# Layer 0's modulation vectors: 48 weight blocks moved from a stage of their own into the two filter stages, with the operands of their matmuls exchanged

## The reference, cut to what matters

```python
def adaln(cvec, w, b):
    m = (jax.nn.silu(cvec) @ w + b)[:, None, :]      # w: 1024 x 6144
    return jnp.split(m, 6, axis=-1)

def hyena_filters(L, lp):                            # L = 256 for the context (C), 512 for the latent (X)
    ...
    h = jnp.sin(freq * (feat @ lp['hy_w1'].astype(f32) + lp['hy_b1'].astype(f32)))
    h = jnp.sin(freq * (h @ lp['hy_w2'].astype(f32) + lp['hy_b2'].astype(f32)))
    h = (h @ lp['hy_w3'].astype(f32) + lp['hy_b3'].astype(f32)).reshape(L, HY_ORDER, 2, HY_WIDTH)
    ...
    taps = taps * lax.rsqrt(jnp.sum(taps * taps, axis=0, keepdims=True) + EPS)
    return jnp.fft.rfft(taps, axis=0)

    for l in range(DEPTH):
        mod = adaln(c, ada_w[l], ada_b[l])
        mod_c = adaln(c_ctx[None, :], ada_w[l], ada_b[l])
        u_c = modulate(rms_norm(ctx, norm1_g[l]), mod_c[0], mod_c[1])
        ...
```

## Time and profile before

| | us |
|---|---|
| median of 3 runs | 5879.87 (5877.63 to 5884.08) |
| the profiled execution | 5873.12 |
| its span, first to last instruction | 5871.3 |
| `stage_ada`, first to last matmul | 19.3 to 117.4 |
| `stage_modulation(0)` | 117.8 to 126.9 |
| filters of C, with the wait for the store | 126.9 to 181.6 |
| filters of X, with the wait for the store | 181.6 to 276.4 |

### The profile page before, as it was taken

One profiled execution on the slowest core, in us unless ns is written; L12 is line 12 of the kernel. 1 busy time (PEld: TensorE's weight loads), 2 busy tenths in 40 slices (PEclk: granted clock), 3 DMA queues, 4 the chain that ended last, 5 costly groups with the idle time before them and its releaser, 6 DMA issues. The chain is left out here.

```text
span 5871.3 us, 69786 instructions
## 1 busy us (share of the span) xinstructions
PE 4953.4 (84%) x23958; PEld 3990.8 (68%) x23958; DVE 4173.0 (71%) x7269; ACT 1841.7 (31%) x3223; POOL 857.5 (15%) x644
## 2 busy tenths in 40 slices
PE   7696737889797869999999778888885679999998
PEld 5385726633575659889888456624764569999997
DVE  1547577768635979999999767667547967676776
ACT  0222312221122753333333211131233733333333
POOL 0000005600000003333333134200000001111110
PEclk9798868999898989999999889989997789999999
DMA  6152317822122669999999467502121367777775
GB/s 225 65 165 75 111 43 274 298 65 65 54 86 90 169 181 386 396 387 400 388 395 391 157 231 269 191 26 82 51 75 52 100 215 272 276 271 277 272 276 189
DMA packets 465588, 1172.70 MB, mean 200 GB/s; under 512 B 225331, under 2 KB 259540, under 8 KB 412438
## 3 DMA queue, kind: packets, MB, share of 16 engines
q1 hardware_dynamic: 373272, 633.88, 32.0%
q0 software_dynamic: 92160, 536.91, 23.9%
HBM read 1106.46 MB, written 64.23 MB: 199 GB/s over the span
## 5 line engine op out<-in xcount | busy, mean ns | idle before, releaser
L2327 POOL DMA_INDIRECT arena<-in_peer_uv,kept x384 | 517.9, 1349 | 3622.1 <-POOLq L2212 1980.2
L232 PE MATMUL psum<-h_hi,u_ring_hi 128*128 128x384 f32 x2048 | 693.6, 339 | 18.4 <-DVE ring_lo L2415 17.9
L232 PE MATMUL psum<-h_hi,ring_lo 128*128 128x384 f32 x2048 | 694.5, 339 | 0.0
L232 PE MATMUL psum<-h_lo,u_ring_hi 128*128 128x384 f32 x2048 | 693.8, 339 | 0.0
L232 PE MATMUL psum<-v_ring_hi,w_hi 128*128 128x512 f32 x1536 | 609.6, 397 | 5.9 <-DVE ring_lo L2420 5.9
L232 PE MATMUL psum<-ring_lo,w_hi 128*128 128x512 f32 x1536 | 603.8, 393 | 0.0
L232 PE MATMUL psum<-v_ring_hi,w_lo 128*128 128x512 f32 x1536 | 600.4, 391 | 0.0
L2420 DVE TENSOR_TENSOR ring_lo<-kept,v_ring_hi 128x1024 fp32r<-128x1024 f32 x256 | 313.8, 1226 | 301.7 <-ACT v_ring_hi L2375 296.5
L2459 DVE SCALAR_TENSOR_TENSOR arena<-arena 128x1024 f32<-128x1024 f32 x384 | 482.1, 1283 | 19.2
L2447 DVE CUSTOM_DVE_ANT_0 arena<-arena 128x1024 f32<-128x1024 f32 x384 | 462.8, 1220 | 29.0 <-DMA arena<-in_peer_uv,kept 28.3
L2387 ACT ACTIVATE w_hi<-arena 128x384 fp32r<-128x384 f32 x256 | 134.7, 526 | 965.3 <-DVE arena L2430 965.3
(11 more groups left out here) (369 smaller groups left out, 10027.7 us busy)
## 6 DMA issues: line engine op xcount, KB each, us to landing
kept<-in_mix SPq DMA_DIRECT2D x312, 512.0 KB, 3.5
kept<-in_peer_u SPq DMA_DIRECT2D x256, 512.0 KB, 5.8
kept<-in_peer_uv SPq DMA_DIRECT2D x256, 512.0 KB, 4.6
kept<-in_ada SPq DMA_DIRECT2D x96, 512.0 KB, 4.4
gate_scratch<-arena SPq DMA_DIRECT2D x12, 4096.0 KB, 20.7
arena<-gate_scratch SPq DMA_DIRECT2D x128, 384.0 KB, 6.0
spec_scratch<-arena SPq DMA_DIRECT2D x4, 2048.0 KB, 8.5
arena<-in_k_dft_x SPq DMA_DIRECT2D x6, 1024.0 KB, 10.2
```

The lines of the kernel that those rows point to most:

```text
L232: done = pe.matmul(out, lhs[x], rhs[y], start=first and j == 0, stop=last and j == 2)
L2327: pool.indirect_dma_start(rows[q % NBUF], None, peer_uv, bass.IndirectOffsetOnAxis(ap=row_id[q % G][:, q // G:q // G + 1], axis=0))\
```

## The change

`stage_ada` is not called any more. For layer 0 its 48 blocks are worked on inside the two filter stages, 24 in each, at named places of TensorE's program (`blocks_beside`): at the beginning 1, behind the first and the second layer 4 each, behind each tile 1, behind the energies of the last tile but one 2, behind spectrum step 2 five, and the rest behind later steps (C: 6 behind step 3; X: one each behind steps 4 to 7). The operands change places: a block's 128 x 128 part is now the stationary operand and `cs` the moving one, with two columns, so each block gives its two columns directly in PSUM bank 7; the copies and the turning matmuls of layer 0 go. The modulation's arithmetic follows the filters and reads PSUM. Its parameters are loaded in the load block, behind the filter weights, and the constants' wait includes them. The wait for C's store goes to DVE's first write of X's spectrum, the wait for X's store into the modulation stage.

```diff
+                load_filter_weights(sp, 0)
+                sp.dma_start(pars, par[0]).then_inc(consts_in.sem, 16)
                 sp.dma_start(fin_g, final_g).then_inc(consts_in.sem, 16)
-                load_filter_weights(sp, 0)
...
-                sp.wait_ge(consts_in.sem, consts_in.at(80))
+                sp.wait_ge(consts_in.sem, consts_in.at(96))
...
             def _(act):
-                act.wait_ge(consts_in.sem, consts_in.at(80))
+                act.wait_ge(consts_in.sem, consts_in.at(96))
...
-        def stage_ada():
+        def pe_ada_column(pe, j):
+
+            k = j % 4
+            pe.wait_ge(loaded[k].sem, loaded[k].at(16 * (j // 4) + 16))
+            for kc in range(KC):
+                last = pe.matmul(ps[:, 7, 2 * j:2 * j + 2], ring[:, k, kc * P:(kc + 1) * P], cs[:, kc, :],
+                                 start=kc == 0, stop=kc == KC - 1)
+            last.then_inc(blocks_done.sem, 1)
...
-            counted_ada()
...
+                if l > 0:
+                    @block.sync
+                    def _(sp):
+                        sp.dma_start(pars, par[l]).then_inc(consts_in.sem, 16)
+                else:
+                    @block.sync
+                    def _(sp):
+                        sp.wait_ge(store_done.sem, store_done.at(0))
...
-                    dve.wait_ge(consts_in.sem, consts_in.at(16))
+                    if l > 0:
+                        dve.wait_ge(consts_in.sem, consts_in.at(16))
...
+                    raw = ada_raw if l > 0 else ps[:, 7, 0:96]
+                    dve.tensor_tensor(mod, raw.rearrange("p (a b) -> p a b", b=2), b, ALU.add)
...
-        def stage_filters(l, s):
+        def stage_filters(l, s, ada_blocks=None):
...
+                    if ada_blocks:
+                        for j in [j for part in ada_blocks.values() for j in part]:
+                            sp.wait_ge(blocks_done.sem, blocks_done.at(j + 1))
+                            sp.dma_start(ring[:, j % 4, :], block_of(order[place[0] + 4 + j])).then_inc(loaded[j % 4].sem, 16)
                     sp.wait_ge(spectrum_made.sem, spectrum_made.at(2 * nt))
...
-                    sp.wait_ge(store_done.sem, store_done.at(32))
+                    if not ada_blocks:
+                        sp.wait_ge(store_done.sem, store_done.at(32))
...
+                    def columns(place):
+
+                        for j in blocks_at(place):
+                            pe_ada_column(pe, j)
+
...
+                    columns("begin")
                     pe.wait_ge(filter_in[0].sem, filter_in[0].at(ready))
                     pe.matmul(ps[0:HID, 4, 0:L], w1[0:EMB, :], feat[0:EMB, :], start=True, stop=True).then_inc(pe_a.sem, 1)
+                    columns("first layer")
                     pe.wait_ge(act_a.sem, act_a.at(1))
                     pe.matmul(ps[0:HID, 5, 0:L], w2[0:HID, :], h1[0:HID, :], start=True, stop=True).then_inc(pe_a.sem, 1)
+                    columns("second layer")
...
+                        columns(("tile", n))
                         if n > 0:
                             energies(n - 1)
+                    columns("last energies")
                     energies(nt - 1)
...
                                 j += 1
+                                columns(("spectrum", j))
...
+                                if j == 0 and ada_blocks:
+                                    dve.wait_ge(store_done.sem, store_done.at(0))
                                 dve.tensor_tensor(stage(o, kt, 0, r), even, odd, ALU.add)
...
-        stage_ada()
+        def blocks_beside(first, tiles, steps):
+            counts = [("begin", 1), ("first layer", 4), ("second layer", 4)]
+            counts += [(("tile", n), 1) for n in range(tiles)] + [("last energies", 2), (("spectrum", 1), 0), (("spectrum", 2), 5)]
+            left = 24 - sum(n for _, n in counts)
+            counts += [(("spectrum", j), left * (j - 2) // (steps - 3) - left * (j - 3) // (steps - 3)) for j in range(3, steps)]
+            counts.append((("spectrum", steps), 0))
+            at = [first + sum(n for _, n in counts[:k]) for k in range(len(counts) + 1)]
+            return {name: range(at[k], at[k + 1]) for k, (name, _) in enumerate(counts)}
         for l in range(DEPTH):
             last = l == DEPTH - 1
-            stage_modulation(l)
             if not last:
-                stage_filters(l, "C")
-            stage_filters(l, "X")
+                stage_filters(l, "C", blocks_beside(0, 2, 4))
+                stage_filters(l, "X", blocks_beside(24, 4, 8))
+                streamed(48, 0)
+                stage_modulation(l)
+            else:
+                stage_modulation(l)
+                stage_filters(l, "X")
             if not last:
                 mixer(l, "C")
                 choose(l, "C")

```

More of the change, by code:

```diff
@@ L402, in _ @@
                 dve.tensor_tensor(cs, cs, cs_sig, ALU.mult)
-        consts_in.add(80)
+        consts_in.add(96)
         act_a.add(1)
@@ L453, in counted_ada @@
             streamed(48, 0)
-        def stage_ada():
[L457 to L474, removed]
-            counted_ada()
+        def pe_ada_column(pe, j):
[5 more added lines that the diff above has]
+            last.then_inc(blocks_done.sem, 1)
         def stage_modulation(l):
             with nc.Block() as block:
-                @block.sync
-                def _(sp):
-                    sp.dma_start(pars, par[l]).then_inc(consts_in.sem, 16)
+                if l > 0:
[6 more added lines that the diff above has]
+                        sp.wait_ge(store_done.sem, store_done.at(0))
                 @block.scalar
@@ L515, in _ @@
                     b = par_of("ada_b").unsqueeze(2).broadcast_to([P, 48, 2])
-                    dve.tensor_tensor(mod, ada_raw.rearrange("p (a b) -> p a b", b=2), b, ALU.add)
+                    raw = ada_raw if l > 0 else ps[:, 7, 0:96]
+                    dve.tensor_tensor(mod, raw.rearrange("p (a b) -> p a b", b=2), b, ALU.add)
                     dve.drain()
@@ L523, in _ @@
                                                      ALU.add, ALU.mult)
-            consts_in.add(16)
+            if l > 0:
+                consts_in.add(16)
             dve_a.add(1)
             act_a.add(1)
-        def stage_filters(l, s):
+        def stage_filters(l, s, ada_blocks=None):
             L = T_OF[s]
@@ L556, in stage_filters, with blocks_at @@
             ready = 80 if l == 0 else 64
+            def blocks_at(place):
+                return ada_blocks[place] if ada_blocks else ()
             MAGIC, TWO_PI = 12582912.0, 2.0 * math.pi
```

## The result

| | median, us | runs | ratio to before, 95% interval |
|---|---|---|---|
| before | 5875.32 (5867.46 to 5895.02) | 8 | |
| after | 5896.21 (5890.82 to 5906.75) | 8 | 1.0036 (1.0024 to 1.0048) |

The change makes the kernel 21 us slower (14 to 28 by the interval), under half a per cent. The forecast was +13 us, 5893, in a range of 5872 to 5908.

The account below looks back on a forecast made before the run. It took TensorE as the engine the filters ahead of layer 0's first norm wait for: 2.0 - 107.6 - 6.5 + 139 - 22.2 + 8 = +12.7 us, so 5880 + 13 = 5893, range 5872 to 5908.

Parts of the forecast that it names:

- Both prices of a block: On TensorE, 16 records of a modulation block take 1.8 us at 2.4 GHz or 3.4 us at 1.2 GHz.
- a busy TensorE was not enough: On TensorE, full moving streams raise the clock; weight loads with two moving columns do not even hold it, despite full busy share.
- The first rival: Clock holds at 2.4 GHz through all 48 blocks, 86 us, and filters' slow parts speed up: -69 us, 5811; chance 6%.
- What went: Ahead of the first norm: 107.6 us before the filters' first matmul and 6.5 us of waiting for C's store go.
- The start: At kernel start, filter weights and parameters landing before the constants are complete add 2.0 us, bounds nothing and 4.
- The number of slow blocks: In both filter stages, about 33 of 48 blocks at 3.4 us and 15 at 1.8 us, together 139 us.
- a sign of being wrong: TensorE waiting for in_ada, the block loads, would prove the forecast wrong; loads were expected to hide, else 4 us once.
- What of it is hidden: Blocks fill TensorE's idle times in the filters of C and X, hiding 22.2 us.
- The neighbours: Filter matmuls beside blocks slow down: C's L579 +2.2, C's last steps +1.6, X's energies +1.1, X's step +3.4; together +8 us.
- the store of X: Ahead of the norm, X's store is still waited for, 11.6 us, with the modulation arithmetic running beside it at no cost.
- "PEclk near 0.5": Sign in the changed profile: granted TensorE clock near 0.5 from about 22 to 55 us, C's beginning, first and second layer.

Follow-up runs that it names:

- the first experiment: The changed kernel with each block's matmuls streaming 128 moving columns, two of cs repeated 64 times, in place of two: 5824.6 us, 0.9917 of before.
- the last experiment: 128 moving columns spread as in the change, plus X's tables behind four block loads, three blocks moved later, half of X's store early: 5806.3 us, 0.9885 of before.
- the third kernel of the table: The changed kernel with the modulation blocks back in their own stage, the rest of the change kept: norm starts at 264.5 us; 5863.6 us, 0.9980 of before.

## Why the prediction was right, point by point

**The number** is in part luck. 5893 was forecast and 5896 measured, but the forecast added 13 us to the 5880 of three runs, and the eight runs of before have 5875; the difference itself was 13 against 21. So the right comparison is that of the sum with the norm's start, 12.7 against 22.0, and it is made here term by term.

**The mechanism** was right. Both prices of a block, read from the turning groups of before, came out: 1.8 and 3.4 us. The argument that a busy TensorE was not enough, from L592's 12.00 us at 0.50, carried over from 65 rows to two columns; the first experiment shows that the width of the stream decides for these blocks. The first rival (6%) was wrong for two columns, and its 69 us are within reach once they are 128: the last experiment has 66 by the norm's start.

**What went** was right within 2 us: the third kernel of the table gives 12 us for what was summed as 13. Of C's store 5.5 us went at the store itself and not 6.5, since TensorE's first block of X starts 1.25 us after the store's issue and not the 0.3 that was estimated for the barrier. But from TensorE's last work in C to the store's issue it was 2.7 us in place of 3.7, so that the whole idle time between C and X went from 10.50 to 3.99, by 6.5 as forecast.

**The start** came 2.1 us later, 2.0 forecast.

**The number of slow blocks** was nearly right: by the starts of the rows the blocks take 142.6 us, 139 forecast. Most of the 3.6 lies in the two groups of five behind step 2, 14.5 us each, in which one or two blocks were fast and not the two or three of the forecast. There was 0.6 us of waiting for a load; such a wait was named as a sign of being wrong, and it showed, but it explains 0.6 us of 22.

**What of it is hidden**, 22.2 us, was right: none of those waits is left, nor one of 0.43 ahead of X's last energies that was not listed. Spreading gave 32.8 in all; the difference is in the main the fast blocks less the slowed neighbours.

**The neighbours** are the term that was too small: 8 forecast. By the starts of the rows C's energies took 12.5 us in place of 8.2 before, X's 20.3 in place of 16.2, C's last two steps 7.3 in place of 5.4 and X's steps 3 and 4, between which no block stands, 2.7 more behind the five blocks: 4.4 + 4.1 + 1.9 + 2.7 = 13. I had counted the clock as up from the first energies on. But behind three of the four groups of one or two blocks that I priced as fast the energies are slow, wholly or in part: C's second (6.37 us for 8 records), X's second (6.72) and X's last (5.38), where only X's third kept its 3.68. That a block just behind 128-row matmuls finds the clock up does not say that the matmuls behind the block do. The experiment without these blocks gave the energies 7.4 of 8.5 us back.

**Small ones**: the store of X ends 12.35 us after its issue in place of 11.59, 0.8 more, with one more stage between. The sum of these is 3.6 for the blocks, 0.6 for the load, 5.0 for the neighbours, 0.8 for the store and 0.1 for the start, less 0.4 for the wait not listed: 9.7, where 22.0 - 12.7 = 9.3 was missed. So more than half of what was missed is the neighbours' term.

**A test of the prediction that misled**: "PEclk near 0.5" from 22 to 55 us. The profile says 1.00 there, ahead of its first recorded change; read as written, this sign would have spoken for the first rival. The test by durations, 16 records in 3.4 us, stands.

## What to carry to other kernels

Before exchanging the operands of a small matmul so that its result comes out turned, look at what then streams: matmuls with a full stationary part and two moving columns left TensorE at 1.2 GHz here, and took the clock from the matmuls behind them too. If the stationary load takes as long as 128 columns would, stream 128 for next to nothing (1.95 us a block in place of 1.84; repeat the operand with a stride of zero) and let the copies fall where later results overwrite them. Work moved into waits should be sized by its price in the clock that it makes itself, and its neighbours priced anew.

## What the runs showed of the hardware

- 768 records with 128 x 128 float32 stationary parts and two moving columns ran for 163.97 us without a gap and never above 1.2 GHz, 213 ns a record; with 128 moving columns the same loads ran at 2.4 GHz but for the first of them, about 113 ns a record. Weight loads with next to nothing streamed did not raise or hold the clock.
- At the upper level a block of 16 records took 1.84 us with two columns and 1.95 with 128 (last matmul's end included): the stream hides behind the load almost wholly.
- The profile's PEclk is 1.00 ahead of the first recorded change, whatever the clock is: over the 164 us above it reads 1.00 at 213 ns a record, and at 57 to 71 us of after it reads 1.00 where eight records of L605 take 7.17 us, the time of a recorded 0.50 before.
